# Moving a kernel's weight buffers and activation buffers to other byte offsets in SBUF

## What is computed

```python
def reference(x, positions, ...):
    h = x
    for layer in range(2):
        h = h + hybrid_mixer(rms_norm(h, attn_norm[layer]), positions, layer, w_in[layer], ..., w_out[layer])
        hn = rms_norm(h, ffn_norm[layer])
        if layer == 0:
            h = h + swiglu(hn, dense_w_gate[0], dense_w_up[0], dense_w_down[0])
        else:
            h = h + moe_ffn(hn, moe_router[0], moe_w_gate[0], moe_w_up[0], moe_w_down[0])
    return rms_norm(h, final_norm)

def swiglu(h, wg, wu, wd):
    return (jax.nn.silu(h @ wg) * (h @ wu)) @ wd
```

## The kernel before

| tensor | start before | start after | past a multiple of 256 B, before / after |
|---|---|---|---|
| `w_hi` | 18432 | 171968 | 0 / 192 |
| `w_lo` | 47104 | 200640 | 0 / 192 |
| `arena_room` | 75776 | 16512 | 0 / 128 |
| `ring` | 139264 | 79744 | 0 / 128 |
| `h` | 188416 | 128896 | 0 / 128 |
| `hn` | 196608 | 137088 | 0 / 128 |
| `hnT_hi`, `hnT_lo` | 204800, 212992 | 145280, 153472 | 0 / 128 |
| `gain` | 221184 | 161664 | 0 / 128 |

## Time and profile before

### The profile page before, as it was taken

One profiled execution on the slowest core, in us unless ns is written; L12 is line 12 of the kernel. 1 busy time (PEld: TensorE's weight loads), 2 busy tenths in 40 slices (PEclk: granted clock), 3 DMA queues, 4 the chain that ended last, 5 costly groups with the idle time before them and its releaser, 6 DMA issues.

```text
span 1539.3 us, 18927 instructions
## 1 busy us (share of the span) xinstructions
PE 1501.2 (98%) x7146; PEld 1247.3 (81%) x7146; DVE 1263.9 (82%) x1564; ACT 1035.2 (67%) x1332; POOL 73.1 (5%) x148
## 2 busy tenths in 40 slices
PE   8989999999998999999999999999999999999996
PEld 7877788888787788888888888888888888888885
DVE  6587555555558799999899999899999899999995
ACT  6464544444355467787787788788788788788784
POOL 4220000000213000000000000000000000000000
PEclk9999999999998899999999999999999999999999
DMA  7511645453342149999999999999999999999992
GB/s 293 197 58 55 239 165 210 172 200 138 123 154 100 57 172 383 374 368 377 354 359 367 362 358 374 350 365 382 350 363 378 344 357 376 363 374 371 365 370 101
DMA packets 181821, 431.61 MB, mean 280 GB/s; under 512 B 3808, under 2 KB 10336, under 8 KB 181728
## 3 DMA queue, kind: packets, MB, share of 16 engines
q1 hardware_dynamic: 180720, 428.01, 75.8%
q10 hardware_dynamic: 1008, 2.36, 0.4%
HBM read 429.31 MB, written 1.05 MB: 280 GB/s over the span
## 4 chain that ended last, share of the span: by engine, by line
PE 91%; DVE 5%; ACT 1%; issue 1%; POOL 1%; DMA 0%; DVEq 0%; POOLq 0%; ACTq 0%
PE pair L865 49%; PE work L865 32%; PE work L837 2%; PE pair L931 2%; PE pair L837 2%; PE work L852 1%; PE work L1109 1%; PE work L1006 1%; DVE w_lo L1510 1%; DVE hn L1502 0%; DVE arena L1569 0%; DVE nmax L1600 0%; PE work L1123 0%; PE work L1124 0%; DVE arena L1586 0%
## 5 line engine op out<-in xcount | busy, mean ns | idle before, releaser
L1510 DVE TENSOR_TENSOR w_lo<-ring,w_hi 128x1024 fp32r<-128x1024 f32 (+3 forms) x810 | 964.6, 1216 | 187.6 <-ACT w_hi L1208 173.9
L1208 ACT ACTIVATE w_hi<-ring 128x1024 fp32r<-128x1024 f32 (+3 forms) x810 | 842.2, 1053 | 309.3 <-PE pair L865 151.4
L865 PE MATMUL pair<-w_hi,hnT_hi 128*128 128x512 f32 x672 | 265.2, 395 | 2.4 <-DVE hnT_lo L1518 1.5
L865 PE MATMUL pair<-w_hi,hnT_lo 128*128 128x512 f32 x672 | 262.2, 390 | 0.0
L865 PE MATMUL pair<-w_lo,hnT_hi 128*128 128x512 f32 x672 | 261.7, 389 | 0.0
L865 PE MATMUL work<-w_hi,hidT_hi 128*128 128x512 f32 x552 | 215.7, 391 | 2.6 <-DVE hidT_lo L1761 1.4
L865 PE MATMUL work<-w_lo,hidT_hi 128*128 128x512 f32 x552 | 215.0, 390 | 0.0
L865 PE MATMUL work<-w_hi,hidT_lo 128*128 128x512 f32 x552 | 215.0, 389 | 0.0
L865 PE MATMUL pair<-w_hi,xU_hi 128*128 128x512 f32 x448 | 177.2, 396 | 0.0
L865 PE MATMUL pair<-w_hi,xU_lo 128*128 128x512 f32 x448 | 174.9, 390 | 0.0
L865 PE MATMUL pair<-w_lo,xU_hi 128*128 128x512 f32 x448 | 174.4, 389 | 0.0
(11 more groups left out here) (214 smaller groups left out, 1366.6 us busy)
## 6 DMA issues: line engine op xcount, KB each, us to landing
ring<-in_moe_w_gate SPq DMA_DIRECT2D x56, 2048.0 KB, 9.8
ring<-in_moe_w_up SPq DMA_DIRECT2D x56, 2048.0 KB, 9.9
ring<-in_moe_w_down SPq DMA_DIRECT2D x56, 2048.0 KB, 9.5
ring<-in_dense_w_gate SPq DMA_DIRECT2D x7, 2048.0 KB, 7.6
ring<-in_dense_w_up SPq DMA_DIRECT2D x7, 2048.0 KB, 7.5
ring<-in_dense_w_down SPq DMA_DIRECT2D x7, 2048.0 KB, 7.8
ring<-in_w_in SPq DMA_DIRECT2D x4, 2048.0 KB, 8.8
ring<-in_w_out SPq DMA_DIRECT2D x4, 2048.0 KB, 9.6
```

Source lines behind the costliest of these rows:

```text
L865: mm = pe.matmul(b, lhs[x_part][k + kk], w[w_part][:, kk, :], start=(first and kk == 0 and i == 0), stop=(last and kk == 1 and i == 2))
L1208: return act.activation(o, i, ACT.Copy)
L1510: dve.tensor_tensor(lo, raw, hi.bitcast(F32), ALU.subtract).then_inc(lo_done, 1)
```

## The change

The declarations are put in another order, and one spacer is 64 floats (256 bytes) shorter. `arena_room` and what shares its bytes now come first, then `ring`, `h`, `hn` and so on, then the small constants and statistics. `w_hi` and `w_lo` come last. `ROWS_ROOM` moves `hn_hi0`, `sel`, `rowsel`, `ident_share` and `share_parts` 256 bytes towards the start of the arena that they share with others. No instruction is added, dropped or given another shape, no semaphore and no wait changes, and the order on each engine is the same.

```diff
-ROWS_ROOM = 4864
+ROWS_ROOM = 4800
...
-        layer_gains = sb("layer_gains", [P, CQ + CKV + 2 * DB])
-        cos = sb("cos", [P, T, NF])
-        w_hi = sb("w_hi", [P, PARTS, 1024], F32R)
-        w_lo = sb("w_lo", [P, PARTS, 1024], F32R)
-
         with nc.sbuf_tensor("arena", [P, ARENA], F32) as arena:
             pass
...
-        mask_q = sb("mask_q", [P, P], BF16)
         ring = sb("ring", [P, RING, SLOT])
         h = sb("h", [P, T, D])
...
         neg_chunk = sb("neg_chunk", [P, CHUNK])
+        mask_q = sb("mask_q", [P, P], BF16)
         mask_k = sb("mask_k", [P, 2 * CHUNK], BF16)
+        cos = sb("cos", [P, T, NF])
+        sin = sb("sin", [P, T, NF])
+        layer_gains = sb("layer_gains", [P, CQ + CKV + 2 * DB])
         cgain, sgain = layer_gains[:, 0:CQ + CKV], layer_gains[:, CQ + CKV:]
-        sin = sb("sin", [P, T, NF])
...
         rope_s = sb("rope_s", [P, HC * DR])
 
 
+        w_hi = sb("w_hi", [P, PARTS, 1024], F32R)
+        w_lo = sb("w_lo", [P, PARTS, 1024], F32R)
```

## The result

The kernel after takes 1556.66 us (median of 8 runs, 1552.75 to 1565.16), and the kernel before 1546.32 us (8 runs, 1541.23 to 1549.23). The two medians are 10.3 us apart. The ratio of the two kernels over all executions is 1.0083, with a 95% interval of 1.0059 to 1.0106, which would be 12.8 us (9.1 to 16.4). I had forecast no effect. The time lies inside my range, on the side of rival 1.

The account below looks back on a forecast made before the run. TensorE's pace was taken as the bound. Removed, added, TensorE, VectorE and ScalarE, and DMA terms were all 0, giving 1541 us against the profiled execution and 1548 as a median, range 1538 to 1567.

Parts of the forecast that it names:

- rival 1: TensorE pays for its operands' start: 1561 us, up to 1574 at 5.2 ns a matmul; chance 0.14.
- What bounds the kernel: TensorE's own pace sets the time, 98% busy; in the experts' stage the DMA engines are nearly full too, at 0.99.
- Removed and added work 0: Whole kernel: no instruction, transfer or wait is removed, added or moved on its engine, so the sum is 0.
- TensorE's reads: Matmul cost of operands starting off a multiple of 256 bytes: bounds 0 and 13 us, 0 taken.
- stricter test: Input-projection matmuls at 328 columns, half misplaced: 0.1488 us measured against 0.1506 on the line, so no cost.
- 416-column row: Input-projection matmuls at 416 columns: 0.1900 us against 0.1874 on the line, 2.6 ns more, or 5.2 if only the misplaced half.
- 2.6 ns x 5016 = 13 us: Upper bound for TensorE: the excess at 416 columns applied to all 5016 matmuls of 512 columns.
- VectorE and ScalarE: Misplaced splits in the experts' stage: up to 9.6 us of VectorE hidden under TensorE; bounds 0 and 1 us, 0 taken.
- DMA: Weight loads landing 128 bytes off: bounds 0 and 3% a load, up to 19 us; 0 taken. The skill's rule gave 39 us.
- Rival 2: DMA engines become the bound of the experts' stage: 1567 us at 3%, 1587 by the skill's rule; chance 0.09.
- rival 3: Faster, since buffers no longer all start at the same place modulo 2048: 1533 us at 3 ns a matmul; chance 0.07.

Follow-up runs that it names:

- e2: Kernel before with everything but the split weights moved by 128 bytes (arena, ring, h, hn, transposed activations): 1576.63 us, ratio 1.0195.
- e3: Changed kernel with two small tensors declared behind the split weights, so the weights start on a multiple of 256: 1575.37 us, ratio 1.0185.
- e4: Kernel before with the split weights alone moved to 128 bytes past a multiple of 256: 1577.38 us, ratio 1.0199.
- e1: Kernel before with the split weights alone moved to 192 bytes past a multiple of 256: 1582.09 us, ratio 1.0224.
- f3: Kernel before with the split weights alone moved to 32 bytes past a multiple of 256: 1580.09 us, one execution.
- f1: Changed kernel with one 64-byte tensor declared behind the split weights, so weights and activations both start at 128: 1546.4 us, ratio 1.0003.
- g2: Kernel before with the weight ring alone moved to 128 bytes past a multiple of 256: 1547.19 us, ratio 1.0003.
- f2: Kernel before with the split weights alone moved to 64 bytes past a multiple of 256: 1555.98 us, ratio 1.0071.
- g1: Kernel before with the low activations alone (hnT_lo, hidT_lo, xU_lo) moved to 128 bytes past a multiple of 256: 1570.96 us, ratio 1.0161.
- g3: Kernel before with w_lo alone moved to 128 bytes past a multiple of 256: 1572.85 us, ratio 1.0182.
- g4: Kernel before with w_hi alone moved to 64 bytes past a multiple of 256: 1581.59 us, ratio 1.022.

## Why the prediction was wrong

*What bounds the kernel.* This was right, with one reading a little too strong: of the last 940 us TensorE is busy for 936.7, and only from 600 to 1500 us is it without a hole. TensorE's own pace sets the time, and 1.8 ns a matmul arrived in full at the end of the stage.

*Removed and added work 0.* Right. Counts, order and waits did not change.

*TensorE's reads.* This is the step that failed: "I take 0, because 328 columns is the stricter test: it is neither on a multiple of 64 nor of 128." The term that I put at 0 measured 1.8 ns for each of 5400 matmuls, 9.7 us, at the changed kernel's distance of 64. Rows narrower than 512 columns do not answer the question. The timeline of the changed kernel shows it at 416, 384 and 512 columns:

```profile
14.33 0.35 PE L864 MATMUL work<-w_lo,hnT_hi 128*128 128x416 f32 x1
...
16.78 0.35 PE L864 MATMUL work<-w_hi,hnT_lo 128*128 128x416 f32 x1
...
22.64 0.34 PE L864 MATMUL work<-w_hi,hnT_hi 128*128 128x384 f32 x1
...
25.06 0.34 PE L864 MATMUL work<-w_hi,hnT_lo 128*128 128x384 f32 x1
...
36.79 0.39 PE L864 MATMUL work<-w_lo,hnT_hi 128*128 128x512 f32 x1
...
40.46 0.39 PE L864 MATMUL work<-w_hi,hnT_lo 128*128 128x512 f32 x1
```

At 416 columns the step is 2.45 / 13 = 0.188 us, at 384 it is 2.42 / 14 = 0.173, both as before within rounding. At 512 it is 3.67 / 16 = 0.229.

The cost has another shape at each width. At 384 columns the mean step in layer 0 is 173.3 ns in the kernel before and at a distance of 64, 175.9 at 128 (e2, e3, e4) and 174.7 at 192 (e1). At 328 columns the misplaced half, 32 bytes off, takes 148.7 ns and the other 150.9, so no cost is seen there. At 512 columns the same 32 bytes cost 6.0 ns (f3). So the "stricter test" says nothing about 512 columns.

The 416-column row that I set aside did hold a cost of placement. Its mean over both halves of a part is nearly the same in all kernels (187.8 to 189.6 ns), because the halves lie 128 bytes apart modulo 256. When the tensors move by 128, one half becomes aligned and the other misplaced. These are the mean steps at 416 columns in layer 0, in the kernels whose weights all have one distance, taken apart by halves:

| distance | it is the first half's, ns | it is the second half's, ns |
|---|---|---|
| 0 | 187.6 (before, f1, g2) | 187.7 (e2, e3, e4) |
| 64 | 190.8 (after, f2) | 190.0 (e1) |
| 128 | 190.6 (e2, e3, e4) | 190.4 (before, f1, g2) |
| 192 | 187.4 (e1) | 187.0 (after, f2) |

Each mean is over 20 to 70 steps and good to some 0.5 ns, and the order of the halves makes no difference. In layer 1 the steps scatter more, and 128 is longer than 0 there too. The excess came from the misplaced half, as I had considered, but with 3 ns and not 5.2. It gives no price for 512 columns either: there, 128 costs 5.5 ns, 64 costs 1.8 and 192 costs 6.1. That 2.6 ns x 5016 = 13 us met the 12.8 us of the ratio is chance, not insight.

I also asked the wrong question of the rows. I took offsets of one operand from a multiple of 256, where the distance between two operands counts. In the rows of the kernel before the two are the same, since its activations start on multiples. In the changed kernel they are not, and the table of starts had it in view: 192 against 128.

*VectorE and ScalarE.* Right, and hidden. VectorE's splits average 1220 ns in the stage, against 1222.

*DMA.* The choice of 0 was wrong for the transfer and right for the time. An isolated load takes 7.8 us where it took 7.5 or 7.6, which is 3 to 4% and so at my bound of 3% or a little above it, and g2 shows that nothing of it reaches the end. The stretch would have needed the arrivals to run dry the split buffers, which did not happen. The rule of the Trainium skill that spoke against the change ("DMA: Bandwidth & Descriptors", "How a descriptor splits into AXI transactions") has the right sign here, and its 39 us did not come.

*Rival 1* named the right engine and the right sign (steps of 0.229 or more with idle times unchanged), with the wrong reason, an operand's own start. *Rival 2* and *rival 3* did not occur. One sign of rival 2 came all the same, dense loads after 7.7 us or more, but not the other two: the experts' gate loads land after 9.6 us and TensorE has no gap. The chance of 0.14 for rival 1 was too low. A unit that does three quarters of the span at one pace deserved more doubt where no row of full width stood at another place.

## What to carry to other kernels

When buffers move, look at the starts of a matmul's moving and stationary operands relative to each other, modulo 256 bytes, and keep that distance at 0. A tensor of 64 bytes in the wrong place cost this kernel 0.8%, and aligning only the weights of the changed kernel (e3) made it slower still, 1.9% above the kernel before. A cost per instruction of the saturated engine is to be bounded only from rows of the same width, and a mean over rows of which half are misplaced is to be taken apart first. And for an effect of under 1%, the distance between the first and the last start of a stage that runs at the full clock repeats to about 0.1%, where the whole span does not.

## What the runs showed of the hardware

The step from one 512-column float32r matmul to the next depends on where the two operands lie relative to each other: 227.2 ns at a distance of 0 modulo 256, 229.0 at 64, and 232.7 to 233.3 at 32, 128, 192 and 224. In the layouts tried it does not depend on where else in SBUF they lie, and 256 bytes more or less make no difference (f1, and g2, whose `hnT_hi` lies 256 bytes further: 227.4 ns both before and there). The mean weight load stays at 187 to 189 ns in all kernels but g1, where it is up to 192. What is longer is the step. The Trainium skill ("SBUF — State Buffer", section "Who interferes with whom") gives TensorE two independent read ports, one for the moving operand and one for the weight load, and says that TensorE never waits on anyone. A cost that depends on the distance between just these two operands is not what that leads one to expect. The measurement decides for the time. That the two reads collide is the natural reading, but it is only argued.

Still open: which pair of accesses meets (g1, g3 and g4 show that neighbouring matmuls take part), why a common distance of 64 is cheap while 32 and 128 are not, and why the cost by distance is smaller and of another shape at 416 columns and fewer. The distances of 96 and 160 were not tried at 512 columns, and 32 and 224 rest on one execution each. No distance that I tried is better than 0, so nothing here beats the kernel before.
